# Samples' attention: one K and V table, groups of eight queries, four queries at a time on the column quarters

## The chip, the cores and the metric

The kernel runs on one core of one Trainium2 chip. The metric is the device time of that core in microseconds (us), the median of several runs. Everything that is told of times comes from these runs and from one profiled execution of the kernel before.

## What is computed

One inference step of a two-layer decoder trunk. Each layer has three parallel head groups (mLSTM, sparse attention, RWKV-7) and a feed-forward network, and runs for a prompt of 1024 tokens and for 64 sample tokens (8 sequences of 8) that have 8192 cached positions behind them. The change touches the sparse attention of the 64 sample tokens. For each token 256 of the cached positions have been selected by an indexer; their K and V rows (4 KV heads of 64, so 256 floats each) are fetched through a page table and attended to:

```python
phys = page_table[bidx, jnp.minimum(idx // PAGE_SIZE, n_pages - 1)]
off = idx % PAGE_SIZE
k_sel = jnp.where(is_new, k[bidx, j], ck[phys, off].astype(k.dtype))
v_sel = jnp.where(is_new, v[bidx, j], cv[phys, off].astype(v.dtype))
s = jnp.einsum('bthgd,btkhd->bthgk', qg, k_sel).astype(jnp.float32) * d ** -0.5
pr = jax.nn.softmax(jnp.where(valid[:, :, None, None, :], s, -jnp.inf), axis=-1)
o = jnp.einsum('bthgk,btkhd->bthgd', pr, v_sel)
```

All arithmetic is in float32.

## The kernel before

A loop over the two layers runs the stages `stage_front` (input projections, indexer, selection), `stage_attend_mix`, `stage_mlstm`, `stage_rwkv`, `stage_prompt_mix` and `stage_mix_ffn`, with a barrier of all engines between them. The change is in `stage_attend_mix` (L3014). It runs two strands of work side by side: `attend_strand` (L2398), the samples' attention, and `mlstm_strand` (L2717), the mLSTM of the prompt in 8 tiles of 18 steps each. A strand is a list of jobs, and each engine's instruction stream is written job by job. `interleave` (L1586) makes one order out of the jobs of both strands from costs that are written in the code (`costs` at the end of each strand), so that both advance at the same share of their total; every engine walks this one order. So an engine that waits in one strand's job also holds back the other strand's next job. The costs of the attend strand are 25 for the start, 2.4 for each of 16 jobs that only find rows, then 2.6, 5.1 and 2.6 for jobs 0 to 15, 16 to 63 and the rest; those of an mLSTM tile add up to 34.5.

A job of the attend strand belongs to one sample token (a query of 8 heads). What the engines do for it:

- **find** (L2500): TensorE multiplies a page selector by the ranks of the pages (two matmuls, L2505). VectorE counts the offsets (L2624), copies the page (L2625), makes the selector of two tokens later (L2618, L2619), and after every fourth token writes the row indices (L2630 to L2632). Finds run 16 tokens ahead of the rest. The next find waits until VectorE has used the last one's bank, so find and count follow each other as a chain.
- **gather** (L2488): GpSimd issues four indirect DMAs for a token, two for K and two for V, of 128 rows of 1 KB each. K goes into a ring of 8 tiles that the transposes free, V, 16 tokens behind K, into a ring of 8 that the value matmuls free.
- **turn** (L2509): TensorE transposes the token's K (four 128x128 transposes, L2514); ScalarE copies it into one of two tiles `kT` (L2585).
- **score** (L2527): two matmuls (L2533) of 128 weight columns by 256 keys. The weight columns are those of a whole group of 16 queries x 8 heads; a diagonal layout `q_diag` holds zeros for the 15 other queries, so that the 16 tokens of a group accumulate in one bank.
- For each group of 16: VectorE masks and takes the maximum (L2664), ScalarE exponentiates (L2589), TensorE transposes the probabilities (L2540, L2541), VectorE lays them out on the diagonal of `p_diag` (L2671, L2672).
- **value** (L2543), `LAG` = 19 jobs behind the turn: two matmuls (L2552) of 128 weight columns of `p_diag` by 256 columns of V. After a group the new rows (L2555), then VectorE's `finish` (L2678 to L2682), and SyncE stores 16 rows (L2478).

There are 84 jobs after the 16 find jobs: turns in jobs 0 to 63, finds in jobs 0 to 47, values in jobs 19 to 82. TensorE's order in a job is turn j, score j-1, find j+16, value j-19.

Of the kernel before, what the change touches and what calls it, by code (L numbers as in the profile page):

```python
# [16 lines left out]
P = 128  # L17
D = 1024
KT = D // P
SEQ = 1024  # L20
# [128 lines left out]
def stage_front(nc, l, io, sc, const):  # L149
# [33 lines left out]
    with Stage(nc) as st:  # L183
# [63 lines left out]
        with nc.Block() as block:  # L247
# [325 lines left out]
            def _(dve):  # L573
# [49 lines left out]
                def place_indices():  # L623
                    rows = float(io["cache_k"].shape[1] * PAGE)
# [1773 lines left out]
def attend_strand(nc, st, l, io, sc, const, bk):  # L2398


    tk = io["cache_k"].rearrange("l n s h d -> (l n s) (h d)")
    tv = io["cache_v"].rearrange("l n s h d -> (l n s) (h d)")
# [3 lines left out]
    STEP = R + BH  # L2406
    NB = 4
    RING = 8
    LAG = 19
# [14 lines left out]
    kb = [st.sb(f"k_sel{n}", [P, 2, KW]) for n in range(RING)]  # L2424
    vb = [st.sb(f"v_sel{n}", [P, 2, KW]) for n in range(RING)]
# [7 lines left out]
    kt = [st.sb(f"kT{b}", [P, 2, TOPK]) for b in range(2)]  # L2433
# [17 lines left out]
    got_k = [st.sem(f"got_k{n}") for n in range(RING)]  # L2451
    got_v = [st.sem(f"got_v{n}") for n in range(RING)]
    stored = [st.sem(f"at_stored{b}") for b in range(2)]
    n_q = lambda t, q: t[:, :, q * R:(q + 1) * R]
    diag = lambda t: t[:, :, :].rearrange("p a (q x) -> p a q x", x=STEP)
    JOBS = NS + LAG + 1
    probs_at = {GQ * (g + 1) + 2: g for g in range(QGROUPS)}
    out_at = {GQ * g + GQ - 1 + LAG: g for g in range(QGROUPS)}

    def sync(sp):  # L2460
# [11 lines left out]
        for j in range(JOBS):  # L2472
            if j - 1 in out_at:
                g = out_at[j - 1]
                sp.wait_ge(y_r, g + 1)
                for q in range(GQ):
                    row = SEQ + g * GQ + q
                    sp.dma_start(sc["y"][row:row + 1, AW:AW + BW].rearrange("o (h d) -> (o h) d", d=HD), o[g % 2][q * BH:(q + 1) * BH, :]).then_inc(stored[g % 2], 16)  # L2478
            yield
        for b in range(2):  # L2480
            sp.wait_ge(stored[b], 16 * GQ * QGROUPS // 2)

    def gpsimd(pool):
        def rows_of(n, table, tiles, got, freed):
            if n >= RING:
                pool.wait_ge(freed, n - RING + 1)
            for f in range(2):
                pool.indirect_dma_start(tiles[n % RING][:, f, :], None, table,  # L2488
                                        bass.IndirectOffsetOnAxis(ap=k_idx[:, n, f:f + 1], axis=0)).then_inc(got[n % RING], 16)

        for n in range(NS + GQ):
            if n < NS:
                if n % NB == 0:
                    pool.wait_ge(k_ready, n // NB + 1)
                rows_of(n, tk, kb, got_k, kt_p)
            if n >= GQ:
                rows_of(n - GQ, tv, vb, got_v, v_used)

    def tensor(pe):
        def find(n):  # L2500
# [3 lines left out]
            for f in range(2):  # L2504
                ins = pe.matmul(p_found[:, f, :], pick[n % 2][:, f * P:(f + 1) * P], rk[:, n, :], start=True, stop=True)  # L2505
            ins.then_inc(found_p, 1)

        def turn(n):
            pe.wait_ge(got_k[n % RING], 32 * (n // RING + 1))  # L2509
            if n >= 2:  # L2510
                pe.wait_ge(kt_r, n - 1)
            for f in range(2):
                for a in range(2):
                    ins = pe.transpose(pt[n % 2][:, a, f * P:(f + 1) * P], kb[n % RING][:, f, a * P:(a + 1) * P], ident[:, :])  # L2514
            ins.then_inc(kt_p, 1)

        def begin(g):
            pe.wait_ge(q_r, g + 1)
            if g:
                pe.wait_ge(mx_r, g)  # L2520
            if g >= 2:
                pe.wait_ge(pd_r, g - 1)
# [13 lines left out]
        def turn_probs(g):  # L2536
            pe.wait_ge(e_r, g + 1)
            pe.wait_ge(biased, min(g + 2, QGROUPS))
# [1046 lines left out]
```

## Time and profile before

| | us |
|---|---|
| median of 3 runs | 6700.14 (6695.44 to 6708.12) |
| profiled execution, its own time | 6708.37 |
| its span | 6706.5 |
| TensorE busy | 5590.6 (83%), mean granted clock 0.865 |
| VectorE busy | 2915.4 (43%) |
| ScalarE busy | 1482.5 (22%) |
| GpSimd busy | 743.1 (11%) |

The span runs from the first to the last instruction of the profiled execution. Busy shares are averages over stages that differ; GpSimd works almost only in two stages of each layer, one of them `stage_attend_mix`. In the first layer that stage has its first DMA at 716.0 and the next stage its first at 1134.3 us of the span; in the second layer they are at 4036.3 and near 4458.

### The profile page before, as it was taken

The numbers are of one execution on the slowest core, as the hardware profiler recorded it, in microseconds if no ns is written. First come the engines' busy times: TensorE is split into PE (matmuls) and PEld (weight loads), VectorE is DVE, ScalarE is ACT, GpSimd is POOL, SyncE is SP. The second block draws the span as 40 slices with busy tenths as digits, with TensorE's granted clock in tenths as the row PEclk, the third lists the DMA queues.
The fourth block names the chain that finished last, engine by engine and source line by source line (L and its number), as shares of the span: only waits on it lengthen the run. The fifth ranks groups of instructions, "written<-read, shape, count | busy, mean of one in ns | idle before, by whom it ended". The sixth has DMA issues, their size and how long they took to land. (4 is left out here: it accounts for less than half of the span.)

```text
span 6706.5 us, 63192 instructions
## 1 busy us (share of the span) xinstructions
PE 5590.6 (83%) x22700; PEld 3464.4 (52%) x22778; DVE 2915.4 (43%) x6694; ACT 1482.5 (22%) x2858; POOL 743.1 (11%) x778
## 2 busy tenths in 40 slices
PE   6999686465789899999989996853757889999997
PEld 4544465244567456654355444642545664666543
DVE  3257563367644233330033666633776442343300
ACT  2310132056243111100033102311553431111000
POOL 2400275000000000000033003730000000000000
PEclk9999688575789999999989996975757889999998
DMA  4222332110000231112132313322000013211122
GB/s 151 88 94 83 79 114 85 38 58 15 11 20 5 116 129 48 57 62 66 52 117 81 115 64 92 111 68 68 27 15 16 15 37 134 85 52 57 59 63 101
DMA packets 358062, 460.05 MB, mean 69 GB/s; under 512 B 75890, under 2 KB 261172, under 8 KB 357332
## 3 DMA queue, kind: packets, MB, share of 16 engines
q1 hardware_dynamic: 320932, 355.93, 16.5%
q0 software_dynamic: 36864, 100.71, 4.9%
q8 instruction: 150, 2.46, 0.1%
q14 instruction: 116, 0.95, 0.0%
HBM read 346.43 MB, written 120.25 MB: 70 GB/s over the span
## 5 line engine op out<-in xcount | busy, mean ns | idle before, releaser
L401 PE MATMUL pp<-w_in,nT 128*128 128x512 f32 x1792 | 806.5, 596 | 0.0
L3255 PE MATMUL pg<-nT,wgu 128*128 128x364 f32 (+1 forms) x2112 | 670.0, 471 | 16.9 <-DMA wgu<-in_w_up 16.9
L3255 PE MATMUL pu<-nT,wgu 128*128 128x364 f32 (+1 forms) x2112 | 665.1, 468 | 0.0
L3325 PE MATMUL pm<-w_down,hT 128*128 128x512 f32 x1408 | 610.0, 596 | 24.1 <-DMA hT<-scratch_hT 24.1
L3255 PEld LDWEIGHTS pg<-nT,wgu 128*128 128x128 f32 x2112 | 403.6, 191 | 261.8 <-issue 21.7
L401 PEld LDWEIGHTS pp<-w_in,nT 128*128 128x128 f32 x1792 | 333.6, 191 | 381.6 <-issue 381.3
L3255 PEld LDWEIGHTS pu<-nT,wgu 128*128 128x128 f32 x2112 | 401.3, 190 | 242.3
L3325 PEld LDWEIGHTS pm<-w_down,hT 128*128 128x128 f32 x1408 | 269.4, 192 | 364.2 <-issue 364.2
L2488 POOL DMA_INDIRECT k_sel<-in_cache_k,kv_idx x256 | 247.4, 966 | 965.1 <-DVE kv_idx L2632 841.0
L3277 DVE TENSOR_SCALAR sig<-exp_neg 128x364 f32<-128x364 f32 x132 | 46.1, 349 | 681.3 <-ACT exp_neg L3266 681.3
L3278 DVE RECIPROCAL exp_neg<-sig 128x364 f32<-128x364 f32 x132 | 319.3, 2419 | 4.5
L3353 DVE TENSOR_TENSOR x_tile<-pm,x_tile 128x512 f32<-128x512 f32 x32 | 22.1, 691 | 612.2 <-PE pm L3325 612.2
L379 POOL DMA_INDIRECT ik<-in_cache_idx_k,idx x256 | 244.3, 954 | 380.1 <-PE pt L436 328.5
L668 DVE TENSOR_SCALAR_CACHE_REDUCE area<-s,cand 128x4160 f32<-128x4160 f32 x62 | 281.9, 4546 | 2.2
L3266 ACT ACTIVATE exp_neg<-pg 128x364 f32<-128x364 f32 x132 | 62.3, 472 | 953.1 <-PE pg L3255 952.8
L2488 POOL DMA_INDIRECT v_sel<-in_cache_v,kv_idx x256 | 246.5, 963 | 96.0 <-issue 73.1
L369 POOL MEMSET iq_diag<- 128x1024 f32 x2 | 1.9, 951 | 2257.5 <-issue 2230.5
L650 DVE COPY ikT<-pt 64x512 f32<-64x512 f32 x128 | 87.4, 683 | 370.0 <-PE pt L436 370.0
L2172 ACT ACTIVATE area<-score,cand 128x768 f32<-128x768 f32 (+2 forms) x192 | 198.0, 1032 | 116.9 <-DVE cand L2321 113.8
L3117 PE MATMUL pm<-w_out,yT 128*128 128x512 f32 x512 | 223.6, 595 | 0.0
L528 ACT ACTIVATE proj<-pp 128x512 f32<-128x512 f32 (+1 forms) x130 | 71.1, 547 | 634.4 <-PE pp L401 628.0
L2111 PE MATMUL bank<-kT,qT 64*128 64x512 f32 (+3 forms) x384 | 179.7, 581 | 24.2 <-DVE mx L2291 24.1
(677 smaller groups left out, 8613.8 us busy)
## 6 DMA issues: line engine op xcount, KB each, us to landing
w_in<-in_w_in SPq DMA_DIRECT2D x14, 2048.0 KB, 9.4
scratch_hT<-hT SPq DMA_DIRECT2D x44, 544.0 KB, 2.7
wgu<-in_w_gate SPq DMA_DIRECT2D x44, 512.0 KB, 3.9
wgu<-in_w_up SPq DMA_DIRECT2D x44, 512.0 KB, 5.1
w_down<-in_w_down SPq DMA_DIRECT2D x22, 1024.0 KB
hT<-scratch_hT SPq DMA_DIRECT2D x16, 1408.0 KB, 7.3
x_all<-scratch_x SPq DMA_DIRECT2D x27, 512.0 KB, 15.5
a_tile<-scratch_pa SPq DMA_DIRECT2D x18, 516.0 KB, 5.1
```

The source lines that it names most:

```text
L379: pool.indirect_dma_start(ring[J % RING][:, f, :, :].rearrange("p o d -> p (o d)"), None, table, bass.IndirectOffsetOnAxis(ap=idx[:, m, 2 ...
L401: ins = pe.matmul(pp[u % 2][:, 0:cw], nT[:, k, t * P:(t + 1) * P], w[:, k, 0:cw], start=(k == 0), stop=(k == KT - 1))
L528: act.activation(pr[u % PR][:, 0:cw], pp[u % 2][:, 0:cw], ACT.Copy).then_inc(chunk_out, 1)
L650: dve.tensor_copy(kt[J % 2][0:HD, :, :], pt[0][0:HD, :, :]).then_inc(kt_r, 1)
L668: dve.tensor_scalar(hit, s[:, :], value, 0.0, ALU.is_ge, ALU.add, accum_out=cnt[:, k:k + 1]).then_inc(counted, 1)
L2111: pe.matmul(bk[n % 2][:, 0:cw], qT[e, kv // 2 * 2 + g, i * P:(i + 1) * P], kT[e, kv // 2, c0:c0 + cw], start=True, stop=True).then_inc(s_p, 1)
L2172: act.activation(rank[:, off[i]:off[i] + width(i)], acc[:, off[i]:off[i] + width(i)], ACT.Sign, bias=cand[:, n:n + 1].bitcast(F32), scale= ...
L2488: pool.indirect_dma_start(tiles[n % RING][:, f, :], None, table, bass.IndirectOffsetOnAxis(ap=k_idx[:, n, f:f + 1], axis=0)).then_inc(got[ ...
L3117: ins = pe.matmul(pm[t % 2][n][:, :], yT[t % 2][:, k, :], w[:, k, n * 512:(n + 1) * 512], start=(k == 0), stop=(k == KT - 1))
L3255: ins = pe.matmul(bank[:, 0:cw], wb[b][:, which, k, :], nT[:, k, c0:c0 + cw], start=(k == 0), stop=(k == KT - 1))
L3278: chain(dve.reciprocal(e[m % 2][:, 0:cw], sg[m % 2][:, 0:cw]))
L3325: ins = pe.matmul(pm[b][n][:, :], h[b][:, k, :], w[:, k, n * 512:(n + 1) * 512], start=(k == 0), stop=(k == FT - 1))
```

## The change

- **One table.** `cache_k` and `cache_v` are handed over as one array `cache_kv`, whose row is a position's 256 floats of K and then its 256 of V. One index gathers both: two indirect DMAs of 128 rows of 2 KB for a token in place of four of 1 KB. They go into one ring of 18 tiles, freed by the value matmuls.
- **Four queries at a time.** Score and value no longer run in every job. Every fourth job one batch takes four tokens: for each half of the contraction four matmuls of 32 weight columns, each for another token and with another moving operand, on the column quarters 0-31, 32-63, 64-95 and 96-127. A quarter holds 4 queries x 8 heads of the group of 16. `token(n)` permutes the order of the tokens so that four that follow each other lie in the four quarters. `kT` has 8 tiles in place of 2.
- **Units of 8.** Mask, maximum, exponential, transposes of the probabilities, `finish` and the stores are done for each unit of 8 queries (8 times a layer) and not for each group of 16 (4 times). Each still works on all 128 rows. `STEP` falls from 136 to 40, so the diagonal tiles shrink from 2 x 2176 to 2 x 640 columns.
- **Order.** `LAG` falls from 19 to 15 and there are 77 jobs after the find jobs in place of 84.

```diff
-    STEP = R + BH
-    NB = 4
-    RING = 8
-    LAG = 19
+    LANES = 4
+    W = R // LANES
+    STEP = W + BH
+    PER = GQ // LANES
+    UNITS = 2 * QGROUPS
+    UQ = GQ // 2
+    BATCHES = PER // 2
+    RING = 18
+    LAG = 15
...
-    JOBS = NS + LAG + 1
-    probs_at = {GQ * (g + 1) + 2: g for g in range(QGROUPS)}
-    out_at = {GQ * g + GQ - 1 + LAG: g for g in range(QGROUPS)}
+    JOBS = NS + LAG - LANES + 2
+    probs_at = {UQ * (u + 1) + LANES + 2: u for u in range(UNITS)}
+    out_at = {UQ * (u + 1) - LANES + LAG: u for u in range(UNITS)}
+
+    def token(n):
+        return n // GQ * GQ + n % LANES * PER + n % GQ // LANES
...
-        for n in range(NS + GQ):
-            if n < NS:
-                if n % NB == 0:
-                    pool.wait_ge(k_ready, n // NB + 1)
-                rows_of(n, tk, kb, got_k, kt_p)
-            if n >= GQ:
-                rows_of(n - GQ, tv, vb, got_v, v_used)
+        for n in range(NS):
+            if n % LANES == 0:
+                pool.wait_ge(k_ready, n // LANES + 1)
             if n >= RING:
-                pool.wait_ge(freed, n - RING + 1)
+                pool.wait_ge(v_used, (n - RING) // LANES + 1)
             for f in range(2):
...
+                pool.indirect_dma_start(kv[n % RING][:, f, :], None, table,
+                                        bass.IndirectOffsetOnAxis(ap=k_idx[:, token(n), f:f + 1], axis=0)).then_inc(got[n % RING], 16)
...
-        def score(n):
-            g, q = n // GQ, n % GQ
-            if q == 0:
+        def score(m):
+            u, g, i = m // BATCHES, m // PER, m % PER
+            if u and m % BATCHES == 0:
+                pe.wait_ge(mx_r, u)
+            if i == 0:
                 begin(g)
-            pe.wait_ge(kt_r, n + 1)
+            pe.wait_ge(kt_r, (m + 1) * LANES)
             for a in range(2):
-                ins = pe.matmul(pS[:, 0:TOPK], n_q(qd, q)[:, a, :], kt[n % 2][:, a, :], start=(q == 0 and a == 0), stop=(q == GQ - 1 and a == 1))
+                for c in range(LANES):
+                    ins = pe.matmul(pS[c * W:(c + 1) * W, 0:TOPK], n_q(qd, c, i)[:, a, :], kt[m % 2 * LANES + c][:, a, :], start=(m % BATCHES == 0 and a == 0), stop=(m % BATCHES == BATCHES - 1 and a == 1))
             ins.then_inc(qk, 1)
...
             for f in range(2):
-                ins = pe.matmul(out, n_q(pd, q)[:, f, :], vb[n % RING][:, f, :], start=(q == 0 and f == 0), stop=False)
+                for c in range(LANES):
+                    ins = pe.matmul(bk[4][c * W:(c + 1) * W, 0:KW], n_q(pd, c, i)[:, f, :], kv[(m * LANES + c) % RING][:, f, KW:2 * KW], start=(m % BATCHES == 0 and f == 0), stop=False)
...
-            if 1 <= j <= NS:
-                score(j - 1)
+            if j % LANES == 0 and 1 <= j <= NS:
+                score(j // LANES - 1)
             if j + GQ < NS:
                 find(j + GQ)
-            if 0 <= j - LAG < NS:
-                value(j - LAG)
+            if (j - LAG) % LANES == 0 and 0 <= j - LAG < NS:
+                value((j - LAG) // LANES)
...
+            if j % UQ == 0 and 1 <= j // UQ <= UNITS:
+                mask_and_max(j // UQ - 1)
+            if j % GQ == 0 and 1 <= j // GQ < QGROUPS:
+                place_queries(j // GQ)
...
-    host = {name: np.ascontiguousarray(inputs[name]) for name in INPUTS}
+    host = {name: np.ascontiguousarray(inputs[name]) for name in INPUTS if name not in ("cache_k", "cache_v")}
+    host["cache_kv"] = np.concatenate([np.asarray(inputs[name]).reshape(DEPTH, -1, PAGE, KVH * HD) for name in ("cache_k", "cache_v")], axis=3)
```

## Rows read from the trace of the kernel before

**Rows 1.** Copies of `kT`: tokens 0, 16, 48 and 63 of layer 1 (start, duration).
```profile
796.71 0.60 ACT L2585 ACTIVATE kT<-bank 128x512 f32<-128x512 f32 x1 [4.35 <-PE bank L2514]
...
847.52 0.60 ACT L2585 ACTIVATE kT<-bank 128x512 f32<-128x512 f32 x1 [1.06 <-PE bank L2514]
...
1013.26 0.60 ACT L2585 ACTIVATE kT<-bank 128x512 f32<-128x512 f32 x1 [2.88 <-PE bank L2514]
...
1077.66 0.60 ACT L2585 ACTIVATE kT<-bank 128x512 f32<-128x512 f32 x1 [2.76 <-PE bank L2514]
```

**Rows 2.** Busy time by stretch: PE, PEld, DVE, ACT, POOL, PE clock, DMA share, GB/s.
```profile
735.00:797.00 62.00, 38.41 (x139) 27.59 (x138) 44.97 (x192) 16.32 (x27) 15.57 (x16) 0.50 0.15 46
797.00:847.50 50.50, 48.65 (x235) 36.25 (x235) 35.31 (x145) 13.94 (x25) 33.09 (x35) 0.79 0.33 100
847.50:1013.30 165.80, 140.39 (x694) 102.46 (x694) 102.02 (x422) 51.98 (x92) 118.73 (x123) 0.89 0.37 110
1013.30:1077.70 64.40, 52.26 (x274) 40.26 (x273) 25.53 (x82) 20.99 (x40) 49.08 (x51) 0.95 0.40 117
1077.70:1122.00 44.30, 36.11 (x155) 24.40 (x153) 15.47 (x48) 10.47 (x19) 30.51 (x33) 0.89 0.35 103
4116.90:4402.30 285.40, 243.46 (x1201) 180.06 (x1202) 163.04 (x649) 87.17 (x156) 201.03 (x209) 0.88 0.37 108
```

**Rows 3.** Waits between 847.5 and 1077.7: total us, times, longest.
```profile
PE bank L2514 <- DMA k_sel<-in_cache_k,kv_idx: 10.0, 8, 2.8
...
POOL v_sel L2488 <- PE bank L2552: 12.1, 8, 5.9
```

**Rows 4.** The gathers' line (min/median/max ns, first and last start); GpSimd's timeline.
```profile
L2488 POOL DMA_INDIRECT k_sel<-in_cache_k,kv_idx x256: 940/946/1412, 760.9 to 4398.3; - x128
...
1099.51 0.95 POOL L2488 DMA_INDIRECT v_sel<-in_cache_v,kv_idx  x1 [0.30 <-issue]
1100.76 0.95 POOL L2488 DMA_INDIRECT v_sel<-in_cache_v,kv_idx  x1 [0.30 <-issue]
```

**Rows 5.** TensorE's timeline where it runs back to back.
```profile
1010.53 0.71 PE L2505 MATMUL bank<-page_ranks,page_of_slot 64*128 64x130 f32 x4
1011.17 1.13 PE L2552 MATMUL bank<-v_sel,p_diag 128*128 128x256 f32 x4
...
1030.43 0.60 PE L2514 MATMUL bank<-c_ident,k_sel 128*128 128x128 f32 x4
1030.87 1.03 PE L2533 MATMUL bank<-kT,q_diag 128*128 128x256 f32 x4
1031.73 1.03 PE L2552 MATMUL bank<-v_sel,p_diag 128*128 128x256 f32 x4
1032.60 0.60 PE L2514 MATMUL bank<-c_ident,k_sel 128*128 128x128 f32 x4
```

**Rows 6.** TensorE's groups between 797 and 1122: busy us, mean ns.
```profile
L2533 PE MATMUL bank<-kT,q_diag 128*128 128x256 f32 x256 | 78.6, 437 | 0.0
L2552 PE MATMUL bank<-v_sel,p_diag 128*128 128x256 f32 x256 | 76.6, 427 | 7.9 <-DMA v_sel<-in_cache_v,kv_idx 6.3 <-DVE p_new L2672 1.5
```

**Rows 7.** Matmuls on column halves elsewhere in the kernel (weights of 64 columns).
```profile
384.92 1.08 PE L399 MATMUL pp<-w_in,nT 128*64 128x256 f32 x8
...
3319.65 19.10 PE L3333 MATMUL pm<-w_down,hT 128*64 128x512 f32 x88
```

**Rows 8.** VectorE's groups between 734 and 1134: busy us, mean ns.
```profile
L2624 DVE TENSOR_SCALAR_CACHE_REDUCE seen<-bank,c_slots 128x128 f32<-128x128 f32 x128 | 44.6, 349 | 79.7 <-PE bank L2505 77.1
L2619 DVE SCALAR_TENSOR_TENSOR page_of_slot<-c_slots,counts_by_page,past 64x256 f32<-64x256 f32 x64 | 30.7, 479 | 2.3
L2618 DVE TENSOR_SCALAR past<-c_slots,counts_by_page 64x256 f32<-64x256 f32 x64 | 22.3, 348 | 0.0
...
L2679 DVE TENSOR_REDUCE o_sum<-o_masked 128x64 f32<-128x256 f32 x4 | 2.4, 588 | 0.1
L2664 DVE CUSTOM_DVE_ANT_0 S<-bank,bias 128x320 f32<-128x320 f32 x4 | 1.9, 482 | 6.3 <-PE bank L2533 6.3
```

**Rows 9.** The last mLSTM tile of layer 1: its first transposes and its output.
```profile
1080.77 0.70 PE L2810 MATMUL bank<-c_ident,a_tile 128*64 128x128 f32 x4
...
1110.73 0.49 DVE L3000 TENSOR_TENSOR y_out<-out_gate,h 128x256 f32<-128x256 f32 x1
```

**Rows 10.** The end of the stage: last output, stores, next stage's first DMA.
```profile
1122.70 0.26 DVE L2682 TENSOR_SCALAR o<-o_sum,mx 128x64 f32<-128x64 f32 x1
...
1126.24 5.34 SPq L2478 DMA_DIRECT2D scratch_y<-o  x16
1134.26 0.35 SPq L826 DMA_DIRECT2D a_tile<-scratch_pa  x1
```

More of the change, by code:

```diff
@@ L623, in place_indices @@
                 def place_indices():
-                    rows = float(io["cache_k"].shape[1] * PAGE)
+                    rows = float(io["cache_kv"].shape[1] * PAGE)
                     chain(dve.tensor_scalar(const["lrow"][:, :], const["lrow"][:, :], rows, None, ALU.add))
@@ L2423, in attend_strand @@
     k_idx = st.sb("kv_idx", [P, NS, 2], U32)
-    kb = [st.sb(f"k_sel{n}", [P, 2, KW]) for n in range(RING)]
-    vb = [st.sb(f"v_sel{n}", [P, 2, KW]) for n in range(RING)]
+    kv = [st.sb(f"kv_sel{n}", [P, 2, 2 * KW]) for n in range(RING)]
     qs = st.sb("q_all", [P, 4, NS])
@@ L2432, in attend_strand @@
     pn = st.sb("p_new", [NS, R])
-    kt = [st.sb(f"kT{b}", [P, 2, TOPK]) for b in range(2)]
+    kt = [st.sb(f"kT{b}", [P, 2, TOPK]) for b in range(2 * LANES)]
     bias = st.sb("bias", [P, NKEY])
@@ L2504, in find @@
             for f in range(2):
-                ins = pe.matmul(p_found[:, f, :], pick[n % 2][:, f * P:(f + 1) * P], rk[:, n, :], start=True, stop=True)
+                ins = pe.matmul(p_found[:, f, :], pick[n % 2][:, f * P:(f + 1) * P], rk[:, token(n), :], start=True, stop=True)
             ins.then_inc(found_p, 1)
         def turn(n):
-            pe.wait_ge(got_k[n % RING], 32 * (n // RING + 1))
+            pe.wait_ge(got[n % RING], 32 * (n // RING + 1))
             if n >= 2:
@@ L2596, in scalar @@
                 turn_in(j)
-            if j % GQ == 1 and 1 <= j // GQ <= QGROUPS:
-                exps(j // GQ - 1)
+            if j % UQ == 1 and 1 <= j // UQ <= UNITS:
+                exps(j // UQ - 1)
             yield
@@ L2617, in pick_pages @@
                 dve.wait_ge(found_p, n - 1)
-            chain(dve.tensor_scalar(past[n % 2][:, :], slot_row[0:NPAGES, :], cT[:, 0, n:n + 1], None, ALU.is_ge))
-            dve.scalar_tensor_tensor(out=pick[n % 2][:, :], in0=slot_row[0:NPAGES, :], scalar=cT[:, 1, n:n + 1], in1=past[n % 2][:, :], op0=ALU.is_lt, op1=ALU.mult).then_inc(pick_r, 1)
+            chain(dve.tensor_scalar(past[n % 2][:, :], slot_row[0:NPAGES, :], cT[:, 0, token(n):token(n) + 1], None, ALU.is_ge))
+            dve.scalar_tensor_tensor(out=pick[n % 2][:, :], in0=slot_row[0:NPAGES, :], scalar=cT[:, 1, token(n):token(n) + 1], in1=past[n % 2][:, :], op0=ALU.is_lt, op1=ALU.mult).then_inc(pick_r, 1)
         def find_offsets(n):
@@ L2623, in find_offsets @@
             for f in range(2):
-                chain(dve.tensor_scalar(seen[:, :], p_found[:, f, 0:PAGE], r1_col[:, f:f + 1], 0.0, ALU.is_lt, ALU.add, accum_out=off[:, n, f:f + 1]))
-            dve.tensor_copy(phys[:, :, n, :], p_found[:, :, PAGE:PAGE + 2].rearrange("p f m -> p m f")).then_inc(found_u, 1)
+                chain(dve.tensor_scalar(seen[:, :], p_found[:, f, 0:PAGE], r1_col[:, f:f + 1], 0.0, ALU.is_lt, ALU.add, accum_out=off[:, token(n), f:f + 1]))
+            dve.tensor_copy(phys[:, :, token(n), :], p_found[:, :, PAGE:PAGE + 2].rearrange("p f m -> p m f")).then_inc(found_u, 1)
         def place_rows(b):
-            q = slice(b * NB, (b + 1) * NB)
-            dve.wait_ge(found_u, (b + 1) * NB)
+            first = token(b * LANES)
+            q = slice(first, first + GQ - PER + 1, PER)
+            dve.wait_ge(found_u, (b + 1) * LANES)
             chain(dve.tensor_tensor(phys[:, 0, q, :], phys[:, 0, q, :], phys[:, 1, q, :], ALU.add))
```

115 lines of the change are left out of this document (52 added, 63 removed).

## The prediction

> **What bounds the kernel now.** I read the page first: TensorE is busy 83% of the span, but the change touches one stage of each layer, so its rows decide. I marked the stage by the copies of `kT`, one for each token [rows 1]: jobs 0 to 15 take 50.8 us, jobs 16 to 47 take 165.7, jobs 48 to 63 take 64.4. From the last turn to the last output [rows 10] it is another 45.0. The table of stretches [rows 2] says what is busy in each. Ahead of job 0, where jobs only find, VectorE is busy 73% and TensorE 62% at a granted clock of 0.50. In jobs 0 to 15 TensorE is busy 96%; in jobs 16 to 47 TensorE is busy 85% and GpSimd 72%; in jobs 48 to 63 TensorE 81%, GpSimd 76%.
>
> GpSimd is fuller than its share says: gathers that follow each other start 1.25 us apart, 0.95 of work and 0.30 of issue [rows 4]. Four gathers for a token are 5.00 us, and jobs 16 to 47 take 165.7 / 32 = 5.18 us each. So GpSimd is at its limit there. TensorE is nearly at its own: the waits [rows 3] show it waiting for K only 10.0 us in 230, and GpSimd waiting for TensorE's value matmuls 12.1. Two engines are close together; faster gathers alone would give little more than those 10 us before job 63. In the tail only GpSimd's V gathers and the value matmuls are left, 2 x 1.25 = 2.5 us a token, beside one mLSTM tile.
>
> **The gathers.** 256 issues in a layer become 128. At 1.25 us that is 160 us in place of 320. The old rows have no gather of 2 KB rows. Bounds: as now, 1.25, if the work goes by rows; 2 x 0.95 + 0.30 = 2.20 us if it goes by bytes, which is 4.4 us a token and 282 us a layer. I take 1.25, since the number of indices is what stays equal. Even at 2.20 GpSimd would be done near 761 + 282 = 1043 us (the first gather is at 760.9 [rows 4]), ahead of the end that I get below, so this term moves the sum little. The ring frees four tokens with value batch m, in job 4m+15, and turn 4m+18 comes three jobs later; at over 3 us a job these are 9 us and more, against 2.5 us of issue for the token. Bytes stay the same. DMA is busy 0.33 to 0.40 there [rows 2], so it doesn't bind.
>
> **Scores and values on quarters.** Back to back at full clock a token's score and its value start 0.87 us before what follows them, its four transposes 0.43 [rows 5]: 2.17 us a token without a find. The two groups hold 78.6 + 76.6 = 155.2 us of TensorE's 277.4 between 797 and 1122 [rows 2, 6]. A batch replaces four tokens' matmuls, 4 x 0.87 = 3.46 us. A matmul leaves two records, so a score is four, 0.22 us each. Quarters aren't in the trace, halves are [rows 7]: 88 records of 512 columns, 44 pairs, in 19.10 us, 0.43 us a pair, where one full-width record of 512 columns would by the 0.22 take as long alone. Eight records of 256 columns on halves take 1.08 us with their end, so 0.87 is their pace too, four pairs at 0.22. Two halves run side by side at no cost. Bounds for a batch: all four side by side 0.87 us, only two 1.73, none 3.46. I take 0.87, as the nearest rows show full overlap. So three quarters of 155 go, 116 us of TensorE in a layer.
>
> What it adds: a change of tile shape. L2505 (64 rows) takes 0.64 us to the next start [rows 5], while four records of 130 columns at 2.4 GHz are 4 x 0.108 = 0.43; two changes cost 0.2, so 0.1 each. A score batch and a value batch have an entry and an exit each; some fall on a change that the find has anyway. That is 0.2 to 0.4 us in four jobs, up to 6 us a layer. The Trainium skill (TensorEngine Tiling (Array Packing), section Tiling Modes) says that a change of mode drains the engine; the trace agrees in that 0.1 us is lost per change, and by that rule the batches pay in full, 6.4 us a layer.
>
> **Units of 8.** Four more units a layer: VectorE's mask 0.48, layout 0.4 + 0.3, finish 0.42 + 0.59 + 0.26 and small ones, 2.7 us a unit, 11 us a layer [rows 8, 10], the layout estimated from the mask, of like width; ScalarE one more exponential, about 0.75, and TensorE three transposes and the new rows, about 0.9 us. They lie in both strands' one order, so I charge 3 us a unit, 12 a layer; bounds 5 and 18. The smaller diagonal tiles shorten two memsets ahead of the stage's work, which lie beside the load of the ranks: nothing.
>
> **What is late next.** VectorE and the order. A find job costs VectorE two counts (0.35 + 0.08 each), a copy 0.16, and the next selector 0.35 + 0.48 [rows 8], with a share of the indices 2.05 us. An mLSTM tile costs it about 13 (25.5 us in jobs 48 to 63, which have no find and some 1.65 tiles by the written costs, less 4 for units [rows 2]). TensorE's own part falls from 2.8 us a find job (0.43 + 0.87 + 0.64 + 0.87) to 1.5. Now by stretch, layer 1:
>
> - Jobs 0 to 15, 50.8 us: VectorE's 35.3 at the 73% that it reaches where it leads (the first of [rows 2]) is 48.4, with a little for the units. Call it 50, gain 1.
> - Jobs 16 to 47, 165.7 us: VectorE's 102.0, plus 7 for two to three units and 2 for the mLSTM share that seven fewer jobs shift here, is 111; at 73% it is 152. By the other way, adding strands: the last mLSTM tile takes 30 us with some nine value jobs in it [rows 9], so about 24 alone; 3.4 tiles x 24 = 82, 32 jobs x 2.1 = 67, units 8, 157. (The same sum for before is 3.25 x 24 + 32 x 2.8 = 168, against 165.7.) I take 153: gain 13.
> - Jobs 48 to 63, 64.4 us: no find. 1.7 tiles x 24 = 41; 16 jobs x (0.43 + 0.43) at a clock near 0.8 are 17; gain 6.
> - The tail, 45.0 us: 13 jobs in place of 20, by the written costs 0.7 of a tile, 17 us; three value batches and a last unit, 7. So 24, gain 21.
> - The last unit stores 8 rows and not 16: half of 5.34 [rows 10], 2.7.
>
> 44 us a layer. Off this 6 for the clock: it is 0.50 at 62% busy and 0.79 to 0.95 at 81 to 96% [rows 2]; TensorE loses 116 us of work, and I expect 0.6 to 0.75 in the stage. 38 us a layer. The second layer has the same stretch at 285.4 us against 280.9, so the same gain. 2 x 38 = 76 off the profiled execution's 6708.4 (span 6706.5 and 1.9 around it) is 6632; the median is 8 lower, so **6625 us**. Its own range is 6590 to 6665.
>
> **Rivals.**
>
> *VectorE packs better and the clock stays up.* In its favour: the find chain loses TensorE's scores and values between two finds. Against: VectorE has 73% at most in a stretch of its own. At 85%: jobs 0 to 15 in 42, 16 to 47 in 131, then 53, 22 and 2.7 less at the end, 79 us a layer: 6543. Chance 0.13.
>
> *The quarters don't overlap.* Then a batch is 3.46 us and TensorE stays the bound to job 63, plus 6 for shape changes and 5 for units, 11 more. The tail still loses its gathers, but not the matmuls, 15, and the store 2.7: 7 us a layer, 6686. For it: no row has a quarter. Against: the halves. Chance 0.11.
>
> *TensorE is left at half clock, and the time rises.* The place is jobs 0 to 63: with three quarters of the score and value work gone, TensorE's load may not hold the clock, and every link through it doubles. At 0.50 a find job is 2 x 1.5 = 3.0 us of TensorE, longer than VectorE's 2.05; a tile is 27, three more for its links through TensorE. Jobs 16 to 47: 3.4 x 27 + 32 x 3.0 = 188, 22 more. Jobs 0 to 15: 0.9 x 27 + 16 x 2.6 = 66, 15 more. Jobs 48 to 63: 46 + 16 x 1.74 = 74, 10 more. Tail 27, 18 less. 29 us a layer more, 6758. It decides once the mean clock of jobs 0 to 63 is below about 0.6. For it: the find jobs' 0.50. Against: an mLSTM tile is about 10 us of TensorE, (52.3 - 16 x 2.17) / 1.65 [rows 2, 5], 20 at half clock, so TensorE would be busy 32 x 3.0 + 3.4 x 20 = 164 of 188 us, 87%, and the stretches that are so busy show 0.79 to 0.95. The Trainium skill (TensorE: Matmul & The Clock Gate, Part 1) has the half rate as the state that only activity releases; by that rule alone the time would be this rival's. The first row of rows 2 bears it out, the others not. Chance 0.10.
>
> The forecast has 0.66. A measurement of this kernel can tell about 0.2%, 13 us, from no change. Faster by more: 0.66 + 0.13 and half of the 0.11, 0.85. Within: the other half, 0.05. Slower: 0.10. The range from 6555 to 6695 takes in the no-overlap case and most of the first rival.
>
> **What would show it.** The gathers: 256 in all, 0.95 us each (up to 1.9 if bytes count), GpSimd busy well under half, no wait of TensorE for them. The quarters: 16 records of a score batch within about 1.0 us at full clock (2.0 at half). Spacing of the `kT` copies about 4.8 us in jobs 16 to 47 and 3.6 in 48 to 63. VectorE's busy share in jobs 16 to 47 up from 62% to about 73%, with TensorE near 60% and the clock between 0.6 and 0.75. From the last turn to the last output some 25 us. I'm wrong if the find jobs stay at 5.2 us though TensorE and GpSimd both idle: then the chain through both strands, not an engine, sets the pace.

## The result, and the profile after

| | before | after |
|---|---|---|
| median of 4 runs each, us | 6704.13 (6695.44 to 6714.53) | 6637.48 (6627.06 to 6650.78) |
| ratio after / before | | 0.9899, 95% interval 0.9884 to 0.9913 |
| span of the profiled execution, us | 6706.5 | 6634.9 |
| mean granted TensorE clock | 0.865 | 0.845 |

The changed kernel is 1.0% faster; the forecast was 6625, the measurement 6637. The profiled spans differ by 71.6 us. After, the stage of layer 1 ran from 714.9 us to its last output, that of layer 2 from 4005.7. By the copies of `kT`, as in [rows 1], its parts are (us):

| | ahead of job 0 | jobs 0-15 | 16-47 | 48-63 | tail | stage |
|---|---|---|---|---|---|---|
| before, layer 1 | 80.7 | 50.8 | 165.7 | 64.4 | 45.0 | 406.7 |
| after, layer 1 | 79.0 | 56.2 | 170.1 | 49.3 | 24.4 | 378.9 |
| forecast, layer 1 | - | 50 | 153 | 58 | 24 | - |
| before, layer 2 | 80.6 | 56.9 | 163.8 | 64.7 | 44.6 | 410.6 |
| after, layer 2 | 78.9 | 57.2 | 174.5 | 43.6 | 24.4 | 378.6 |

The row of the forecast is before its 6 us for the clock, which it took off the stage as a whole. The stages gave 27.8 + 32.0 us and the shorter last stores 2 x 2.7, 65 us together. Some 6 us more lie in stages that the change doesn't touch, and I don't attribute them. But for 1.7 us a layer ahead of job 0, all of the gain is behind job 48. Jobs 0 to 47, where three quarters of the score and value work also went, became slower: by 9.8 us in layer 1 and 11.0 in layer 2.

The copies of `kT` for tokens 0, 16, 48 and 63 of layer 1, on ScalarE's timeline after (they answer to [rows 1]):

```profile
793.87 0.60 ACT L2586 ACTIVATE kT<-bank 128x512 f32<-128x512 f32 x1 [5.73 <-PE bank L2514]
...
850.05 0.60 ACT L2586 ACTIVATE kT<-bank 128x512 f32<-128x512 f32 x1 [0.90 <-PE bank L2514]
...
1020.16 0.60 ACT L2586 ACTIVATE kT<-bank 128x512 f32<-128x512 f32 x1 [5.14 <-PE bank L2514]
...
1069.49 0.60 ACT L2586 ACTIVATE kT<-bank 128x512 f32<-128x512 f32 x1 [0.42 <-PE bank L2514]
```

The busy time by stretch after, with the columns of [rows 2]: PE, PEld, DVE, ACT, POOL, PE clock, DMA share, GB/s.

```profile
735.00:794.00 59.00, 37.80 (x139) 27.68 (x140) 42.70 (x178) 15.66 (x27) 23.48 (x24) 0.50 0.38 112
793.90:850.00 56.10, 50.72 (x245) 34.69 (x249) 39.50 (x170) 17.09 (x31) 12.24 (x13) 0.57 0.26 76
850.00:1020.20 170.20, 133.20 (x731) 85.72 (x734) 107.05 (x439) 51.30 (x96) 64.11 (x67) 0.64 0.40 113
1020.20:1069.50 49.30, 40.81 (x270) 25.79 (x270) 27.37 (x92) 25.06 (x45) 24.56 (x26) 0.71 0.56 162
1069.50:1093.90 24.40, 18.36 (x137) 11.04 (x137) 14.46 (x45) 5.85 (x12) 0.00 (x0) 0.77 0.02 6
```

Read the third row against its like in [rows 2]. GpSimd fell from 118.7 us busy to 64.1, so it no longer binds. TensorE has 133.2 in place of 140.4, hardly less, at a clock of 0.64 in place of 0.89. In the second row the clock is 0.57 where it was 0.79.

TensorE's groups from 794 to 1094, by form (busy us, mean ns, idle before), beside [rows 6]:

```profile
L2514 PE MATMUL bank<-c_ident,kv_sel 128*128 128x128 f32 x252 | 57.3, 372 | 0.3 <-ACT kT L2586 0.3
L2505 PE MATMUL bank<-page_ranks,page_of_slot 64*128 64x130 f32 x192 | 50.1, 403 | 16.8 <-DVE slot_page L2626 16.6
L2553 PE MATMUL bank<-kv_sel,p_diag 128*32 128x256 f32 x256 | 25.7, 544 | 0.5 <-DVE p_new L2675 0.5
L2534 PE MATMUL bank<-kT,q_diag 128*32 128x256 f32 x256 | 24.6, 519 | 0.0
```

The scores and values hold 50.3 us; in [rows 6] it was 155.2. That is 105 us less, and the forecast had 116. But TensorE's whole busy time in jobs 0 to 63 and the tail fell only by 34 us, from 277.4 (four stretches of [rows 2]) to 243.1. The time of a group runs to the end of its last record and overlaps the next group, so the groups add up to more than the busy time: 312 us before, 264 after. Without scores and values they are 157 us before and 213 after, 56 more. Some 9 of that are the groups that the units of 8 repeat (L2541, L2542, L2556). The other 47 are the same records as before, each of them longer: the transposes L2514 take 57.3 us and were 44.1, the finds L2505 50.1 and 38.8. The mean clock of these stretches fell from 0.88 to 0.65, which by its own ratio would make 44.1 into 60 and 38.8 into 53 (an estimate). So the lower clock took back somewhat under half of what the quarters freed.

The quarters themselves, on TensorE's timeline: a score batch at full clock, then a value and a score batch at half. The second column is from the first start to the last end of the 16 records:

```profile
915.86 1.06 PE L2514 MATMUL bank<-c_ident,kv_sel 128*128 128x128 f32 x4
916.85 1.15 PE L2534 MATMUL bank<-kT,q_diag 128*32 128x256 f32 x16
917.92 0.38 PE L2505 MATMUL bank<-page_ranks,page_of_slot 64*128 64x130 f32 x1
...
928.67 1.93 PE L2553 MATMUL bank<-kv_sel,p_diag 128*32 128x256 f32 x16
930.53 1.12 PE L2514 MATMUL bank<-c_ident,kv_sel 128*128 128x128 f32 x4
931.58 1.94 PE L2534 MATMUL bank<-kT,q_diag 128*32 128x256 f32 x16
```

16 records take 1.15 us with their end where 16 full-width ones took 4 x 0.87 [rows 5]. To the start of what follows it is 1.07 us at full clock and 1.86 at half, against 0.87 and 1.73 for four quarters wholly side by side. The 0.13 to 0.20 us more fit the forecast's 0.1 for each of two changes of shape, which no run isolates. Beside 3.46 us the overlap is all but complete.

The gathers' line on the page, and what GpSimd and VectorE wait for between 850 and 1020 (total us, times, longest):

```profile
L2496 POOL DMA_INDIRECT kv_sel<-in_cache_kv,kv_idx x256 | 248.9, 972 | 1193.8 <-DVE kv_idx L2634 853.7
```

```profile
POOL kv_sel L2496 <- PE bank L2553: 123.9, 9, 35.5
...
DVE seen L2625 <- PE bank L2505: 49.6, 16, 6.4
...
PE bank L2505 <- DVE slot_page L2626: 12.3, 7, 3.5
```

A gather of 128 rows of 2 KB is 972 ns of GpSimd in the mean and 946 at the median; those of 1 KB took 966 and 963 (K and V) in the mean and 946 at the median [rows 4]. GpSimd now idles until value batches free the ring. TensorE's matmuls wait for no gather in layer 1, where it was 10.0 us [rows 3], and 1.8 us in layer 2. The waits that lead are those of the find chain: the count waits for the find's matmuls 49.6 us, the next find for the count 12.3. The first of the two isn't new. In the kernel before it is, in the same jobs (847.5 to 1013.3):

```profile
DVE seen L2624 <- PE bank L2505: 54.2, 20, 6.9
```

So the change took the scores' and values' time off TensorE, and VectorE waits for the find nearly as long as before.

The end of the stage, after: the last two mLSTM tiles' outputs, the last output of attention, its store (8 rows) and the next stage's first DMA, as in [rows 9, 10]:

```profile
1063.76 0.43 DVE L3002 TENSOR_TENSOR y_out<-out_gate,h 128x256 f32<-128x256 f32 x1
...
1092.25 0.42 DVE L3002 TENSOR_TENSOR y_out<-out_gate,h 128x256 f32<-128x256 f32 x1
...
1093.87 0.25 DVE L2685 TENSOR_SCALAR o<-o_sum,mx 128x64 f32<-128x64 f32 x1
...
1097.41 2.65 SPq L2484 DMA_DIRECT2D scratch_y<-o  x8
1102.73 0.35 SPq L826 DMA_DIRECT2D a_tile<-scratch_pa  x1
```

The last tile takes 28.5 us from output to output, and attention's last output comes 1.6 us behind it. So attention is hidden beside that tile; before, its last output came 12 us after the tile's [rows 9, 10].

### The profile page after: what moved, and what is told of

Its sections match the earlier page's. It is cut to its first block and busy times, and to the rows that moved or that the text cites. A ratio compares the mean times of both kernels' runs of the same rounds, so it can differ in the third digit from the quotient of the medians.

```text
span 6634.9 us, 63216 instructions
## 1 busy us (share of the span) xinstructions
PE 5522.5 (83%) x22818; PEld 3365.9 (51%) x22818; DVE 2922.8 (44%) x6766; ACT 1486.3 (22%) x2874; POOL 496.1 (7%) x522
## 5 line engine op out<-in xcount | busy, mean ns | idle before, releaser
L2496 POOL DMA_INDIRECT kv_sel<-in_cache_kv,kv_idx x256 | 248.9, 972 | 1193.8 <-DVE kv_idx L2634 853.7
L2505 PE MATMUL bank<-page_ranks,page_of_slot 64*128 64x130 f32 x512 | 141.1, 421 | 62.4 <-DVE slot_page L2626 61.7
```

The costliest lines, as they stand in the source:

```text
L2496: pool.indirect_dma_start(kv[n % RING][:, f, :], None, table, bass.IndirectOffsetOnAxis(ap=k_idx[:, token(n), f:f + 1], axis=0)).then_inc( ...
```

## The experiments

The questions: what of the change brings the gain, why jobs 0 to 47 didn't get faster, and whether that can be mended. Two views of the same cause were held against each other: that the lower clock itself gives the gain back, so that more matmuls would help, and that the chain of find, count and next find sets the pace, through whatever TensorE has in front of a find.

The runs were made in three groups, each on another chip. The kernel before took 6880.13 us (median of 9) on that of the first, 6862.03 (9) on that of the second and 6710.51 (16) on that of the third; only the last is like the chip of the result. The third chip is the only one of that kind that any edit ran on. Ratios are to the kernel before on the same chip.

### The cache as two tables

```diff
-            for f in range(2):
-                pool.indirect_dma_start(kv[n % RING][:, f, :], None, table, ...).then_inc(got[n % RING], 16)
+            for part, table in ((0, tk), (1, tv)):
+                for f in range(2):
+                    pool.indirect_dma_start(kv[n % RING][:, f, part * KW:(part + 1) * KW], None, table, ...).then_inc(got[n % RING], 16)
```

Everything else stays as after: quarters, units of 8, one ring.

> The changed kernel with its gathers undone alone: K and V are again two arrays, four indirect DMAs of 1 KB rows for a token into the two halves of the same ring tile. Theory A (the single table matters): 256 issues of 1.25 us are 320 us a layer from 759, so the last turn can't come before about 1080 (1069.5 in the changed kernel), and with the waits for the ring jobs 16 to 63 take 5 us each where 48 to 63 take 3.1 now. 10 to 30 us a layer more, 6660 to 6700 in all. Theory B (TensorE's work was the bound, the gathers only looked full): the last turn stays within 5 us of 1069 and the time within 10 us of the changed kernel's 6637.

Measured 6998.87 us, ratio 1.0172 (1.0149 to 1.0196): slower than the kernel before. The expectation was for a chip like the result's and doesn't hold on this one. Jobs 16 to 47 took 251.9 us. What is late shows in the waits between 900 and 1240, where "remote" is a release later than the end of anything that the profile shows, and in the timeline from 1157:

```profile
ACT kT L2588 <- remote: 138.7, 13, 20.5
POOL kv_sel L2498 <- PE bank L2555: 137.2, 11, 30.3
DVE seen L2627 <- remote: 88.5, 12, 17.2
```

```profile
1157.45 1.09 PE L2516 MATMUL bank<-c_ident,kv_sel 128*128 128x128 f32 x8
1158.61 0.95 POOL L2498 DMA_INDIRECT kv_sel<-in_cache_v,kv_idx  x1 [0.30 <-issue]
...
1168.77 0.95 POOL L2498 DMA_INDIRECT kv_sel<-in_cache_v,kv_idx  x1 [0.30 <-issue]
1169.81 0.42 DVE L2992 TENSOR_TENSOR CT<-bank,CT 64x260 f32<-64x260 f32 x1 [6.39 <-remote]
...
1172.58 0.60 ACT L2588 ACTIVATE kT<-bank 128x512 f32<-128x512 f32 x1 [19.45 <-remote]
1173.07 0.55 ACT L2592 ACTIVATE S<-S,mx 128x320 f32<-128x320 f32 x1
1173.29 0.72 PEld L2516 LDWEIGHTS bank<-c_ident,kv_sel 128*128 128x128 f32 x4 [14.98 <-issue]
```

The transposes end at 1158.5 and ScalarE copies them at 1172.6, though it has nothing to do. In between GpSimd issues gathers back to back. From job 0 of this layer to the stage's end there are 108 us in which neither TensorE nor VectorE nor ScalarE is busy, counting only gaps over 0.8 us; on the chip of the result it is 1 us before and none after. The two stages took 552.3 and 549.5 us, against 406.3 and 405.7 of the kernel after on its like chip (below): 290 us for 256 issues more, 1.1 us each. The forecast's sum had 1.25 us of GpSimd for an issue, but most of it hidden beside the other engines; on this chip hardly any of it is hidden. So this run doesn't show what the single table is worth on a chip like the result's, and no other does.

### The quarters' loop order

```diff
-            for a in range(2):
-                for c in range(LANES):
+            for c in range(LANES):
+                for a in range(2):
```

The same in `value`. It was meant to make the matmuls of one quarter follow each other and so to take the overlap away.

> The changed kernel with the two loops of a batch exchanged: both matmuls of a quarter, then the next quarter's. A quarter's second matmul waits for its first, so a batch should take about five matmul times in place of two, 2.2 us at full clock in place of 0.87; 32 batches, 41 us of TensorE more a layer. If TensorE's work sets the pace (theory A), each layer is 30 to 40 us longer, 6700 to 6717. If the chain between the two strands and the clock set it (theory B), the granted clock of jobs 16 to 47 rises from 0.64 to 0.75 or more, these jobs stay at 170 us within 8, and the time is 6640 to 6665.

6724.52 us, ratio 0.9780 (0.9756 to 0.9805). The overlap stayed; TensorE's timeline at full clock has

```profile
1081.10 0.60 PE L2514 MATMUL bank<-c_ident,kv_sel 128*128 128x128 f32 x4
1081.63 1.09 PE L2534 MATMUL bank<-kT,q_diag 128*32 128x256 f32 x16
```

1.09 us, as in the kernel after, and the ratio is that of the kernel after on its like chip (0.9778, below). The expectation had a quarter's second matmul wait for its first and hold up the next quarter; it doesn't. The edit removed nothing, and this way of asking what the overlap is worth failed. The answer came with the four times repeated batches below.

### One more matmul in each find job

```diff
+            if n + GQ < NS:
+                pe.matmul(bk[n % 2][:, 0:256], ident[:, :], masks[:, 0:2, :], start=True, stop=True)
             for f in range(2):
                 for a in range(2):
                     ins = pe.transpose(...)
```

Its result is overwritten by the transposes.

> The changed kernel with one more matmul (identity by 256 float32 columns, its result overwritten) ahead of the transposes in each of the 48 jobs that have a find: 0.43 us at full clock, 21 us a layer. Theory B (the low clock gives the saved TensorE time back in jobs 0 to 47): the granted clock there rises from 0.57 and 0.64 to 0.75 or more, jobs 16 to 47 fall from 170 to 155 to 165, and the time to 6610 to 6630. Theory A (every TensorE instruction lies on the chain, the clock hardly answers): 0.43 to 0.85 us a job more, 20 to 40 us a layer, 6680 to 6715.

6746.10 us, ratio 0.9817 (0.9797 to 0.9837). The kernel after itself was run on the next chip, of the same kind.

### Before and after once more, on a chip of that kind

> The kernel before, unchanged, for its profile on the chip of this call: the last call's chip ran it in 6880 us and not in 6700. If the cause is in the chip, the 180 us more lie in the stage with the gathers, as moments in which all engines stand still while gathers are under way; the other stages stay within 10 us.

> The changed kernel, unchanged, beside the others of this call. On a chip like the first: 0.990 of before. On a chip like the last call's, where each burst of gathers holds the engines up, half as many gathers should bring more than on the first: 0.970 to 0.980.

One run of the unchanged kernel took 6846.77 us. The changed kernel took 6700.75, ratio 0.9778 (0.9758 to 0.9797): here the change is worth 161 us and not 67. The stages before were 488.7 and 482.0 us, against 406.7 and 410.6 on the chip of the result; after they are 406.3 and 405.7, against 378.9 and 378.6. The waits of the kernel before between 862 and 1075 on this chip show why:

```profile
POOL v_sel L2488 <- PE bank L2552: 54.6, 12, 17.7
DVE seen L2624 <- PE bank L2505: 48.9, 14, 7.5
DVE seen L2624 <- remote: 36.0, 8, 8.7
ACT kT L2585 <- remote: 26.0, 6, 6.5
```

The "remote" waits are there with four gathers a token, and fewer with two. Of the 128 `kT` copies 34 start over 2 us after their transposes' end in the kernel before and some 15 in the kernel after; with two tables it was about 50. On the chip of the result it is none and 2.

With this the extra matmul can be read. The stretches of jobs 0 to 15 and 16 to 47, first the kernel with it, then the kernel after on its like chip:

```profile
795.60:851.30 55.70, 52.48 (x277) 36.64 (x281) 39.19 (x167) 17.11 (x31) 13.01 (x13) 0.72 0.24 69
851.30:1056.90 205.60, 146.87 (x792) 97.03 (x795) 106.84 (x437) 51.99 (x95) 63.26 (x67) 0.69 0.33 93
```

```profile
797.30:849.50 52.20, 45.38 (x245) 30.82 (x249) 39.47 (x170) 17.02 (x31) 12.26 (x13) 0.66 0.26 74
849.50:1037.60 188.10, 137.92 (x731) 90.01 (x734) 107.66 (x438) 51.81 (x96) 62.92 (x66) 0.63 0.35 101
```

The clock rose from 0.63 to 0.69, and jobs 16 to 47 became 17.5 us longer (21.9 in layer 2). 32 matmuls of that shape are 14 us at full and 28 at half clock, by the halves of a score in [rows 5]. So work put in front of the find is paid in these jobs at about its own length, and the higher clock doesn't return it. That speaks against the view that more matmuls would help. It doesn't tell the find chain from a plain sum of TensorE's work, which would be longer by the same. The Trainium skill (TensorE: Matmul & The Clock Gate, Part 1) has the full rate as what activity releases; the trace agrees, but here the activity costs more than the rate gives.

### The find first in its job

```diff
         for j in range(JOBS):
+            if j + GQ < NS:
+                find(j + GQ)
             if j < NS:
                 turn(j)
             if j % LANES == 0 and 1 <= j <= NS:
                 score(j // LANES - 1)
-            if j + GQ < NS:
-                find(j + GQ)
```

> The changed kernel with TensorE's find moved ahead of the turn and the score in a job. In jobs 16 to 47 VectorE waits 49.6 us for TensorE's find. Theory B (the hand-off find, count, next find through both engines sets the pace of these jobs): the turn and the batches then run beside VectorE's count; the waits fall to 25 us or less, jobs 16 to 47 from 170 to 145 to 160, the time to 6590 to 6620. Theory A (it is the sum of the work or the mLSTM chain): no stretch changes by more than 5 us, the time stays within 10 us of 6637.

> TensorE's find ahead of turn and score, against the changed kernel on the same chip. Theory B (the hand-off of find and count sets the pace of jobs 16 to 47): 10 us a layer or more less in these jobs, 20 to 60 us in all. Theory A (these jobs take one mLSTM tile's own chain, 28 us for 9.4 jobs, plus VectorE's 2.05 us a job, one after the other): TensorE's order in the job changes nothing, within 10 us of the changed kernel.

6694.43 us, ratio 0.9734 (0.9721 to 0.9748), and on the second chip 6698.51, ratio 0.9748 (0.9730 to 0.9765), beside 0.9778 for the kernel after on that chip. The intervals overlap: 2 us less by the medians, some 20 by the ratios. Jobs 16 to 47 of layer 1 are shorter in both, here the first:

```profile
857.00:1038.40 181.40, 131.72 (x726) 83.35 (x724) 106.79 (x435) 51.85 (x95) 63.10 (x67) 0.66 0.37 106
```

181.4 us against the 188.1 of the kernel after, but jobs 0 to 15 and the part ahead of them took 5.7 more, and on the second chip layer 2 gained nothing in this stretch (185.2 and 185.1). The count's wait for the find's matmuls fell from 44.7 us in the kernel after to 27.0, and only 6.7 of these 17.7 us came off the stretch. The two stages together are no shorter, 815 and 817 us against 812. The expectation for the second chip had 10 us a layer or more for the chain and at most 10 us in all against it: layer 1 lies between, layer 2 and the medians say that the order changes nothing. The sign in layer 1 is that of the chain, the size small.

### More work on VectorE in each find

```diff
             chain(dve.tensor_scalar(past[n % 2][:, :], slot_row[0:NPAGES, :], cT[:, 0, token(n):token(n) + 1], None, ALU.is_ge))
+            chain(dve.tensor_scalar(past[n % 2][:, :], slot_row[0:NPAGES, :], cT[:, 0, token(n):token(n) + 1], None, ALU.is_ge))
```

0.34 us for each of 128 tokens: 43 us of VectorE in all.

> The changed kernel with the first of the two selector instructions of VectorE done twice with the same result, 0.35 us more for each of 62 tokens. Theory A (VectorE's work for a find adds to the mLSTM tile's chain): most of it shows, 0.25 to 0.40 us a job in all find jobs, 30 to 50 us in all. Theory B (VectorE waits for TensorE's find 50 us in jobs 16 to 47 and would have the time): under 12 us.

6724.55 us, ratio 0.9792 (0.9774 to 0.9810). By the medians that is 24 us over the kernel after, by the ratios 10. The profile has 13.4 and 14.8 us more in jobs 16 to 47, and 47 in the two stages together (432.6 and 426.7 us):

```profile
854.70:1056.20 201.50, 143.57 (x730) 92.70 (x734) 117.84 (x470) 51.74 (x95) 62.12 (x66) 0.59 0.33 94
```

VectorE has 10.2 us more in this stretch and the stretch is 13.4 longer, with VectorE busy 58%. So time added on VectorE in the find job shows in the profile in full, though VectorE idles four tenths. By the profile this is the expectation's theory A, that VectorE's work for a find adds to the tile's. The ratio alone doesn't settle it, since its interval reaches that of the kernel after.

### The third chip: the batches four times, and gathers held back

`e_four_times` repeats each batch's matmuls four times, and so gives TensorE the time of full-width ones back, with all the rest of the change in place. Scores and values come out four times too large.

```diff
-            for a in range(2):
+            for a in range(8):
                 for c in range(LANES):
-                    ins = pe.matmul(..., n_q(qd, c, i)[:, a, :], kt[...][:, a, :], ...)
+                    ins = pe.matmul(..., n_q(qd, c, i)[:, a % 2, :], kt[...][:, a % 2, :], ...)
```

The same in `value`. `e_paced` lets GpSimd gather a token only when the gathers two tokens earlier have landed:

```diff
+            if n >= 2:
+                pool.wait_ge(got[(n - 2) % RING], 32 * ((n - 2) // RING + 1))
             for f in range(2):
                 pool.indirect_dma_start(...)
```

`e_paced_find` is that with the find first.

> The changed kernel once more, unchanged, as the measure for the other three of this call. 0.990 of before on a chip like the first, 0.978 on one like the last two.

> The changed kernel with the matmuls of each score and value batch done four times over into the same sums, so that a batch holds TensorE as long as the full-width matmuls did, 3.46 us at full clock in place of 0.87; scores and outputs come out four times too large. Everything else, the gathers too, is as in the changed kernel. Theory A (the quarters bring the gain: TensorE's time lies in the chain of jobs to 63): most of the 83 us a layer comes back, less what a higher granted clock saves, 80 to 160 us in all over the changed kernel, so the kernel before or slower. Theory B (the halved gathers and the shorter tail bring it): less than 50 us over the changed kernel.

> The changed kernel with GpSimd held to two tokens' gathers in flight: before a token's gathers it waits until those of the token before the last have landed. Theory A (on chips where engines see each other's semaphores late, it is the pile of gathers in flight that holds them up): the delays from the last transpose to ScalarE's copy that exceed 2 us, 13 to 20 of 128 there, fall to 5 or fewer, and the time falls by 15 to 50 us; on a chip like the first nothing changes. Theory B (each gather costs its delay however they are spaced): within 10 us of the changed kernel.

> The pacing and TensorE's find at the head of the job together. If pacing and order each bring what I think, 20 to 60 us below the changed kernel on a chip like the last two, 0 to 20 on one like the first. If neither does, within 10 us of it.

| | median, us | ratio to before (95%) | jobs 16-47, layers 1, 2 | stages |
|---|---|---|---|---|
| after | 6655.02 | 0.9921 (0.9895 to 0.9947) | 170.2, 166.1 | 378.7, 368.6 |
| four times | 6731.75 | 1.0034 (1.0017 to 1.0051) | 197.0, 197.0 | 425.0, 425.2 |
| paced | 6651.61 | 0.9909 (0.9895 to 0.9924) | 172.0, 168.6 | 382.2, 376.6 |
| paced, find first | 6620.96 | 0.9869 (0.9854 to 0.9884) | 160.1, 163.5 | 375.2, 372.1 |

Four times: jobs 16 to 47, and TensorE's two groups from 793.5 to 1140, in which the batches now hold 134.1 us, near the 155.2 of [rows 6]:

```profile
858.50:1055.50 197.00, 163.23 (x1498) 103.83 (x1495) 104.36 (x428) 51.51 (x96) 61.98 (x66) 0.77 0.34 97
```

```profile
L2553 PE MATMUL bank<-kv_sel,p_diag 128*32 128x256 f32 x1024 | 69.4, 432 | 0.7 <-DVE p_new L2675 0.7
L2534 PE MATMUL bank<-kT,q_diag 128*32 128x256 f32 x1024 | 64.7, 410 | 0.0
```

Without the quarters' saving the kernel is 77 us slower (6731.75 - 6655.02), just under the 80 to 160 expected, and 21 slower than before. On this kind of chip all the rest of the change together brings nothing, half the gathers among it, and the quarters bring more than the whole gain. By stretch the rest does both: jobs 48 to 63 took 53.5 us and the tail 30.8, against 64.4 and 45.0 before, while jobs 0 to 47 took 262 against 216.5. No run takes back the gathers, the units of 8 or the new order alone on such a chip, so how these 25 us of gain and 46 of loss divide among them isn't shown. Jobs 16 to 47 took 197 us with TensorE busy 163 at a clock of 0.77, where the kernel before had 166 with 140 busy at 0.89 [rows 2]. Not all of that loss need be the change's: the repeated batches come in lumps of 64 records, which the kernel before didn't have.

Pacing alone changes nothing here, as expected for such a chip. Paced and with the find first, the kernel takes 34 us less than after by the medians, more than the 0 to 20 expected, and the intervals don't touch. Jobs 16 to 47, and the first wait of VectorE in them:

```profile
858.60:1018.70 160.10, 134.47 (x726) 86.13 (x730) 104.58 (x425) 52.12 (x96) 62.70 (x66) 0.64 0.41 120
```

```profile
DVE seen L2627 <- PE bank L2507: 30.4, 16, 5.0
```

The same wait is 49.6 us in the kernel after and 52.3 in the paced one. With the same work at the same clock (0.64) and 10 us less, these jobs of layer 1 fit the chain made shorter. But the stages as a whole hardly are: the two of this kernel sum to 747.3 us, 12 less than the paced kernel's, and just as much as those of the kernel after (368.6 in its second layer is the shortest of all). The profiled executions differ by 17.5 us in all. Behind layer 2's stage, in what neither edit touches, the kernel after took 2281.6 us and this one 2257.8; the paced kernel took 2241.4 there. So a stretch that is the same in all three differs by more than the executions do, and the 34 us can't be put down to the chain.

## Why the prediction was right, step by step

- **Gathers at 1.25 us by their count: right.** 256 in all, 972 ns each with twice the bytes, and TensorE's matmuls wait 1.8 us for them in the two layers together. The bound of 2.20 by bytes fell. That faster gathers alone would give little fits the four-times kernel, which has them and all the rest but not the quarters' saving; alone they were run on no chip of this kind.
- **Batches at 0.87: right**, 1.07 to the next start at full clock with its changes of shape, and 1.15 with the end where eight records on halves took 1.08. The rival of no overlap is out, and so is an order of issue that matters. The 0.1 us for a change of shape wasn't isolated.
- **6 us for the clock: mis-sized, and put down without a sum.** The clock came to 0.57 in jobs 0 to 15 and 0.64 in 16 to 47, at the low end or below the 0.6 to 0.75 of the forecast, and TensorE's other work grew by 56 us in layer 1, about 47 of them in the same records. TensorE was 78% busy in jobs 16 to 47, not 60%. This is the mechanism of the rival that came out slower. Its deciding value was 0.6 for jobs 0 to 63; the mean of the three stretches, weighted by their lengths, is 0.64. Its price for jobs 0 to 15, 15 us more, was too high (5.4 and 0.3), for 16 to 47, 22 more, too (4.4 and 10.7), and jobs 48 to 63 became shorter, not 10 longer.
- **Jobs 16 to 47 at 153: wrong, 170.1 and 174.5.** The sum took VectorE's 73% from the stretch of finds alone. It reached 63%. The mark for being wrong had been find jobs at 5.2 us with TensorE and GpSimd idle; they are at 5.3, with GpSimd idle 62% and TensorE 22%. So no single engine is the limit. That it is the find chain is shown only in part. A matmul in front of the find was paid in full and 10 us more on VectorE gave 13 more, but a plain sum of both strands' work would give the same. The find first, which alone tells the two apart, gave 7 to 12 us less in layer 1 and 0 to 5 in layer 2 (the paced kernels' difference is the larger). The other sum, tile by tile, failed in one term: the last tile is 28.5 us from output to output in the tail at a clock of 0.77, not 24. 3.4 x 28.5 = 97 and the sum's own 8 for units leave 65 for 32 jobs, 2.0 each, against the 2.1 of the forecast (2.2 in layer 2). That is a fit, not a measurement, but if the last tile stands for those before it, the slower tile alone accounts for these jobs.
- **Jobs 48 to 63 at 58: 49.3 and 43.6.** The 17 us that the forecast added for the jobs' own matmuls weren't there: a tile took 33 us from output to output (1030.5 to 1063.8), where the last one took 28.5. Jobs without a find are mostly hidden beside a tile.
- **The tail at 24: 24.4 in both layers**, though by another way: the value batches and the unit, priced at 7 us, are hidden but for 1.6, and what is left of the tile behind the last turn takes 22.8 us (1069.5 to 1092.3), not 17.
- **VectorE packs better and the clock stays up (6543):** neither happened. (Its parts add up to 81 us a layer and not 79, which is 6539.)

So 38 us a layer came out as 27.8 and 32.0 with 2.7 each for the stores, 65 us in place of 76. That it is so near is in good part luck: a gain too large by 17 to 24 us in jobs 16 to 47 stood against one too small by 9 to 15 in jobs 48 to 63. And without the 6 us from stages that the change doesn't touch, the forecast would have missed by 18 us and not by 12.

## What to carry to other kernels

When work is taken from a busy TensorE, price what is left of it at the clock that it will then have: here 105 us of matmuls went and some 47 came back in the same records at a lower clock. Where several strands share in-order engines, look beside the busy shares for waits between engines that the change leaves standing: "the count waits for the find" was 54 us in these jobs before and 50 after. Putting the find first in its job took 18 to 22 us off that wait and 7 to 12 off the jobs of one layer, but between the pairs of profiles the two stages together changed by 12 us less to 5 more. Narrow weight groups on column quarters can be worth a batch's extra work where four independent products can be had at once. And a change of 1% needs the kernel before beside it on the same chip.

## What the runs showed of the hardware

- Sixteen float32 records of 256 columns on four column quarters take 1.07 to 1.15 us with their end at full clock, whichever of the two loops is outside, and 1.93 at half; sixteen full-width ones took 3.46 to the next start. The Trainium skill (TensorEngine Tiling (Array Packing), Tiling Modes) says that tiles work independently; the trace agrees.
- An indirect gather costs GpSimd the same for rows of 2 KB as of 1 KB (946 ns at the median in both, 972 and 965 in the mean).
- Chips differ by more than this change is worth, and not alike for every kernel. The kernel before took 6704 and 6711 us on two and 6862 and 6880 on two others, and nearly all of it lies in the stage with the gathers: 488.7 us against 406.7. While gathers are issued back to back there, engines start up to 20 us after what they wait for has ended, and for 32 us (the kernel before) to 108 (two tables) of layer 1's stage none of TensorE, VectorE and ScalarE is busy. What causes it is not settled. It grows from two gathers a token to four in the same kernel, but those two were run on different chips, and pacing the gathers was run only on a chip without it, where it changed nothing.
